# Half of the rope's squares go behind the block sums, and a table says how many rope slices follow each sum

## What is computed

```
h = _rmsnorm(x, norm_gain[l])
proj = h @ w_in[l]
q_a, k_a, v_a, g_a, q_b, k_b, v_b, g_b = jnp.split(proj, split_at, axis=-1)
q_a = _rmsnorm(q_a.reshape(b, s, A_HEADS, HEAD_DIM), q_norm_a[l])
k_a = _rmsnorm(k_a.reshape(b, s, A_KV_HEADS, HEAD_DIM), k_norm_a[l])
q_a = q_a * cos + _rotate_half_axial(q_a) * sin
k_a = k_a * cos + _rotate_half_axial(k_a) * sin
...
o_a = _gqa_blocked(q_a, k_a, v_a) * jax.nn.silu(g_a)
```

## Time and profile before

| what | value |
|---|---|
| three timed runs | 1477.88, 1477.89, 1478.12 us; median 1477.89 |
| the profiled execution's own time | 1478.08 us |
| span of its profile | 1476.3 us (1.78 us of the time lie around it) |
| PE busy | 1425.7 us, 97% of the span |
| DVE busy | 902.3 us, 61% |
| ACT busy | 631.1 us, 43% |
| POOL busy | 485.4 us, 33% |

### The profile page before, as it was taken

The page is one execution under the profiler, slowest core; times in us unless marked ns, Lnnn a source line. Parts: engine busy times, 40 slices in busy tenths (PEclk is TensorE's granted clock), DMA queues, the critical chain, the costliest instruction groups (busy, mean ns, idle before and its releaser), DMA issues.

```text
span 1476.3 us, 30658 instructions
## 1 busy us (share of the span) xinstructions
PE 1425.7 (97%) x12538; PEld 1257.1 (85%) x12538; DVE 902.3 (61%) x1535; ACT 631.1 (43%) x1251; POOL 485.4 (33%) x554
## 2 busy tenths in 40 slices
PE   7998989989999999999999999999998998999998
PEld 7998988867788788888899999888897887888887
DVE  6899971349999888745520633452424776888431
ACT  5422321137777677633432122332335554777210
POOL 0176641310000277622202212221205884434420
PEclk9999999999999999999999999999999999999999
DMA  6303346000000033256325245433121121222342
GB/s 234 115 15 94 101 152 123 29 1 1 1 1 1 28 116 95 81 178 180 85 44 59 54 91 94 53 64 50 30 69 41 31 90 43 66 81 63 101 134 80
DMA packets 89937, 109.50 MB, mean 74 GB/s; under 512 B 25215, under 2 KB 71967, under 8 KB 89800
## 3 DMA queue, kind: packets, MB, share of 16 engines
q1 hardware_dynamic: 89800, 107.55, 27.8%
HBM read 82.30 MB, written 25.22 MB: 73 GB/s over the span
## 4 chain that ended last, share of the span: by engine, by line
PE 58%; DVE 4%; ACT 1%; issue 1%; POOL 0%; DVEq 0%; ACTq 0%
PE ps L393 23%; PE ps L1812 12%; PE ps L3317 2%; PE ps L1620 2%; PE ps L1604 2%; PE ps L3303 2%; PE ps L3292 1%; PE ps L2693 1%; PE ps L2636 1%; PE ps L2651 1%; PE ps L1597 1%; PE ps L1598 1%; PE ps L1599 1%; PE ps L3280 1%; PE ps L3293 1%
## 5 line engine op out<-in xcount | busy, mean ns | idle before, releaser
L359 POOL TENSOR_TENSOR p_w_lo<-p_w_raw,p_w_hi 128x2048 fp32r<-128x2048 f32 (+1 forms) x21 | 103.5, 4927 | 394.0 <-ACT p_w_hi L332 394.0
L393 PE MATMUL ps<-p_w_hi,w_out_hi 128*128 128x256 f32 (+1 forms) x640 | 180.9, 283 | 0.1
L393 PE MATMUL ps<-p_w_lo,w_out_hi 128*128 128x256 f32 (+1 forms) x640 | 180.4, 282 | 0.0
L393 PE MATMUL ps<-p_w_hi,w_out_lo 128*128 128x256 f32 (+1 forms) x640 | 180.4, 282 | 0.0
L393 PEld LDWEIGHTS ps<-p_w_hi,w_out_hi 128*128 128x128 f32 x640 | 121.0, 189 | 0.9 <-issue 0.6
L393 PEld LDWEIGHTS ps<-p_w_hi,w_out_lo 128*128 128x128 f32 x640 | 121.1, 189 | 0.0
L393 PEld LDWEIGHTS ps<-p_w_lo,w_out_hi 128*128 128x128 f32 x640 | 120.4, 188 | 0.0
L332 ACT CAST p_w_hi<-p_w_raw 128x2048 fp32r<-128x2048 f32 (+1 forms) x22 | 42.0, 1909 | 124.1 <-DMA p_w_raw<-w_in 93.1
L1325 DVE TENSOR_TENSOR a_pt_lo<-ps,a_pt_hi 128x512 fp32r<-128x512 f32 x128 | 82.2, 683 | 15.3 <-ACT a_pt_hi L1376 15.3
L1376 ACT CAST a_pt_hi<-ps 128x512 fp32r<-128x512 f32 x128 | 68.9, 590 | 45.8 <-PE ps L1266 45.8
L1368 ACT ACTIVATE tok<-ps,a_stat 128x1024 f32<-128x1024 f32 x64 | 72.5, 1132 | 22.7 <-DVE a_stat L1320 22.7
(11 more groups left out here) (348 smaller groups left out, 4282.1 us busy)
## 6 DMA issues: line engine op xcount, KB each, us to landing
p_w_raw<-w_in SPq DMA_DIRECT2D x20, 1024.0 KB, 9.0
kbT<-x SPq DMA_DIRECT2D x8, 512.0 KB, 6.9
p_w_raw<-w_in SPq DMA_DIRECT2D x8, 512.0 KB, 4.3
b_w_raw<-w_out SPq DMA_DIRECT2D x8, 512.0 KB, 3.6
qT<-s_gate SPq DMA_DIRECT2D x8, 512.0 KB, 6.9
qT<-x SPq DMA_DIRECT2D x8, 512.0 KB, 3.5
s_x<-qT SPq DMA_DIRECT2D x8, 512.0 KB, 2.8
c_table<-s_line SPq DMA_DIRECT2D x8, 512.0 KB, 3.9
```

The lines of the kernel that those rows point to most:

```text
L359: ops.tensor_tensor(self.w_lo[:, b, :, 0:w], self.raw[:, :, 0:w], self.w_hi[:, b, :, 0:w].bitcast(F32), ALU.subtract).then_inc(self.w_lo_r ...
L393: last = self.nc.tensor.matmul(out, lhs, rhs, start=(kt == 0 and i == 0), stop=(kt == KT - 1 and i == 2))
```

## The change

The squares of tiles 0 to 3 and `place_second_sum` stay where they are. The squares of tiles 4 to 7 (with the scale behind the last) become a generator, `square`, chained ahead of `rope`, and the sums no longer wait for them. How many slices follow sum n is in a table: row 0 for group 0, row 1 for groups 1 and 2.

```
         pr.first_vector(dve, sv.first_sum)
         sv.prepare_vector(dve)
-        for t in range(NT):
-            if t == NT // 2:
-                sv.place_second_sum(dve, pr.chunk_end(STD - 1))
...
-        turning = rope(dve, step)
-        for _ in sv.evacuate(dve):
-            for _ in range(2):
-                next(turning, None)
-        for _ in turning:
+        squares = square(dve, step)
+        for t in range(NT // 2):
+            next(squares)
+        sv.place_second_sum(dve, pr.chunk_end(STD - 1))
+        work = one_after_other(squares, rope(dve, step))
+        for n, _ in enumerate(sv.evacuate(dve)):
+            for _ in range(SLICES[min(n // 10, 1)][n % 10]):
+                next(work, None)
+        for _ in work:
             pass
...
+    SLICES = ((1, 1, 0, 2, 0, 0, 1, 1, 1, 2), (2, 1, 0, 2, 1, 2, 2, 2, 2, 2))
+
+    def one_after_other(*works):
+        for work in works:
+            yield from work
+
+    def square(dve, step):
+        for t in range(NT):
+            dve.wait_ge(pr.emptied["act"], 2 * NT + t + 1)
+            x = qkv[:, t, 0:NH * HD]
+            step(nc.vector.tensor_tensor(tmp[:, :], x, x, ALU.mult))
+            step(nc.vector.tensor_reduce(stat[:, 0, t * NH:(t + 1) * NH],
+                                         tmp[:, :].rearrange("p (h d) -> p h d", d=HD), AX.X, ALU.add))
+            if t == NT - 1:
+                nc.vector.tensor_scalar(stat[:, 0, :], stat[:, 0, :], 1.0 / HD, EPS, ALU.mult, ALU.add).then_inc(var_ready, 1)
+            yield
```

## The result

The change makes the kernel faster by 0.73%: 1467.24 us (1466.04 to 1468.55, four runs) against 1477.97 us for the kernel before in the same session (1477.88 to 1478.12, four runs), a ratio of 0.9927 with a 95% interval of 0.991 to 0.9945. The profiled execution took 1467.59 us, its span 1465.8. The forecast was 1465.8 us, with a range of 1464.5 to 1470.5.

A forecast was written before the change was run, and what follows sets the result against it. PE, busy 97% of the span, was taken as the bound, with stalls waiting for DVE's L813. From 1478.08 us, 13.05 for both stalls came off and 0.8 for thin places was added: 1465.8 us, range 1464.5 to 1470.5.

The forecast's parts named there:

- The two stalls: PE's waits for L813 at product 4 of groups 0 and 2: both go, 13.05 us with their slow matmuls.
- The start of group 0: Ahead of product 4 of group 0: first L813 at about 106, wanted at 112.9, so the first stall goes.
- the margin of 0.9 us: Group 1's weights: second `low` ends at 135.0, PE wants it at 135.9; nothing charged, 2 us at most.
- Groups 1 and 2: Group 1's L813 at 149 to 153 and last L826 at 173 to 183; no stall there, second stall goes.
- its limit of 182.4: Latest start of group 1's last L826 that has STD's weights ready when PE wants them at 210.4.
- the part on the rest: After group 2: rope and L420 evictions hidden; second q_b chunk's L359 1.0 us ahead of PE, 1 us at most.
- all four thin places: Group 1's weights, its L813, STD's weights, second q_b chunk: each could lose up to 2 us; 0.8 charged in all.
- the likeliest case: Both stalls go and at most 2 us are lost: 1464.8 to 1467.3 us, chance 62%.
- Rival 1: A new stall of 1.5 to 5 us at L813 of group 1 or 2, or STD: 1467.5 to 1472, 23%.
- Rival 2: The stall at L813 of group 2 stays, DVE as far behind as before: 1470.6 plus up to 3, chance 6%.
- Rival 3: Little or no effect, squares still standing ahead of the first L813: 1475 to 1481 us, chance 4%.
- rival 4: DVE's backlog at group 1's last L826 delays STD's weights, making the kernel slower: 1481 to 1485 us, chance 3%.

The follow-up runs named there:

- experiment 5: The changed kernel itself run again, unedited, on a second chip: 1467.42 us, ratio 0.9927 to the kernel before.
- experiment 3: Changed kernel with the table undone: squares moved, but two slices behind every sum, as before; 1473.4 us, ratio 0.9975.
- 9: Changed kernel with three more slices ahead of the first L813 of group 1, taken from behind it; 1468.76 us, ratio 0.9934.
- 4: Changed kernel with all eight squares back ahead of the sums, only the slice table kept; 1473.81 us, ratio 0.9974.
- experiment 10: Changed kernel with group 2's two slices behind n = 26 split, one behind n = 25, one behind n = 27; 1464.39 us, ratio 0.9909.
- 1: Changed kernel with the two slices ahead of group 2's second L822 moved behind it; 1464.48 us, ratio 0.9912.
- 2: Changed kernel with the second q_b chunk's weight load issued ahead of the table loads on SP; 1464.7 us, ratio 0.9913.
- 6: Changed kernel with group 2's two slices behind its second L822 and the second q_b chunk's load ahead of the table loads; 1464.26 us, ratio 0.9905.
- 7: Changed kernel with four slices behind n = 26 and none behind n = 27, so four precede group 2's second L822; 1471.01 us, ratio 0.995.

## Why the prediction was right, and what it missed

**The two stalls.** Right, in mechanism and size: 13.05 us forecast, 13.31 measured. The forecast said that the changed profile would show no wait for L813 above 0.5 us; it shows none at all. It also said that there would be no window of half clock between 90 and 260, and that sign failed: the eight matmuls from 234.46 ran slow, with 0.79 granted over 232 to 240. STD's first matmul came at 209.79 (210 to 212 forecast), but the end did not move by as much: 13.7 us earlier at STD, 10.5 at the end.

**The start of group 0.** Right in kind. The DVE rows there:

```profile
98.75 0.69 DVE L806 TENSOR_TENSOR tok<-tok,ps 128x512 f32<-128x512 f32 x1 [0.81 <-ACT tok L777]
99.36 1.78 DVE L1111 TENSOR_TENSOR rope_tmp<-tok 128x640 f32<-128x640 f32 x1
...
104.96 0.69 DVE L813 TENSOR_TENSOR f_v<-tok,ps 128x512 f32<-128x512 f32 x1
106.94 0.69 DVE L813 TENSOR_TENSOR f_v<-tok,ps 128x512 f32<-128x512 f32 x1 [1.29 <-PE ps L766]
```

The first L813 came at 104.96 (106.1 forecast), the second at 106.94 and waiting for PE. The timelines of ACT and POOL, with the root, the fourth emptying of X and group 1's weights:

```profile
114.66 0.27 ACT L1039 ACTIVATE rope_stat<-rope_stat 128x80 f32<-128x80 f32 x1 [6.61 <-DVE rope_stat L1115]
118.47 0.38 ACT L786 ACTIVATE p_spill<-ps 128x256 f32<-128x256 f32 x1 [1.30 <-DMA s_gate<-p_spill]
...
127.25 2.98 POOL L627 TENSOR_TENSOR p_w_lo<-p_w_raw,p_w_hi 128x1024 fp32r<-128x1024 f32 x1
```

The root was at 114.66 ("near 115"). The second `low` ended at 130.2 where 135.0 was the worst and 132 to 135 the working value, so the margin of 0.9 us was 5.2 in fact (wanted at 89.60 + 8 x 5.72 = 135.4). The forecast's reason, that the wait for the store would take up a part of the delay, holds: ACT's fourth emptying of X started at 118.47 after 1.30 us where it had waited 4.27, so of the root's 4.3 us only 0.6 were left. Whether the store shared the DMAs with two weight loads, as the forecast had it, no run tests.

**Groups 1 and 2.** The pair of L813 of group 1 started at 148.65 (149 to 153 forecast), wanted from 152.5. The last L826 of group 1 started at 179.97. That is inside the stated 173 to 183 but past the 173 to 177 of the working, and 2.4 us ahead of its limit of 182.4. DVE's first and last sum of group 1:

```profile
139.37 0.69 DVE L806 TENSOR_TENSOR tok<-tok,ps 128x512 f32<-128x512 f32 x1
...
179.97 0.68 DVE L826 TENSOR_TENSOR tok<-tok,ps 128x512 f32<-128x512 f32 x1
```

Both times hold two misses that cancel, and that is luck. ACT's copy started at 138.58, earlier than the forecast's 141 to 145, and the slices were dearer than its 1.9 us. The three ahead of L813 took 8.1 us where 5.7 were charged. From L806 to L826 were 40.6 us where 32.0 were forecast; 3.5 of them DVE waited for PE, which leaves (40.6 - 3.5 - 5.4)/14 = 2.3 us a slice. From a copy at 141 to 145 the same way would have ended some 2.4 to 6.4 us later, about at the limit of 182.4 or past it, unless those 3.5 us of waiting had taken up a part. STD's weights were there at 201.58 + 4.60 = 206.2, 3.6 us early. The two L813 of group 2 came at 185.67 and 187.08, wanted from 192.6. There the forecast's sum has a slip: it names five slices and adds four. With five it is 11.3 us from L826, and the late end of 183 would have missed its 193.2 by 1. In the run POOL was idle from 179.30 to 185.17, so no slice was held up, and the whole way took 5.7 us.

**The term that was mis-sized** is the last of the part on the rest: "That L359 itself ends 1.0 us ahead of PE's job at 245.78 and hangs on SP's queue behind table loads that move with PE; I charge nothing, 1 us at most." The place was named and the slack was right (0.97). But what the loads move with is the `c12` store, and so DVE's L822, with PE only as long as no slice holds L822. The forecast looked at L806, L813 and L826 and never at L822, which in the trace of before waited 2.19 us for PE and so looked safe. Behind it the new table still has two slices between the two L822, where the rope of before had been used up after n = 24, and POOL's 4.6 us L359 falls just there. The part of the sum for all four thin places was 0.8 us; this one alone cost 3.9 in the profiled execution and 2.6 in another (experiment 5). From the profiled time of before, the sum with what was measured is 1478.08 - 13.31 - 0.38 + 3.88 - 0.7 = 1467.6, where 1467.59 was measured: 3.1 too little was charged, and 1.3 of it came back by more won (0.3), an earlier start (0.4) and the 0.7 elsewhere, none of which the forecast had a reason for. The median of 1467.24 lies just inside the likeliest case, 1464.8 to 1467.3, although that case's condition, at most 2 us lost, did not hold. That is luck.

**The rivals.** Rival 1 (a smaller new stall, "1467.5 to 1472") describes the size of the stall that came but not the place: it named L813 and STD. Experiments 3 and 9 show that its mechanism is real and near. Rival 2 (the second stall stays) is excluded: no wait. Rival 3 (little effect) and rival 4 (slower) did not come; experiments 3 and 4 show that it takes both halves to come near the whole gain.

**The shared port.** The Trainium skill (SBUF — State Buffer, "Who interferes with whom") says that a DVE instruction with two SBUF inputs and a POOL instruction that reads SBUF exclude each other for a whole instruction. The trace agrees: 4.63 us against 0.69 for one L1152, behind and ahead of POOL's L359 (changed kernel and experiment 10), while the sums that read PSUM kept 0.67 to 0.69 us throughout. The forecast's rival 1 and its late end priced what waits in group 1 with POOL's 2.4 us; at the place that mattered POOL's instruction is 4.6 us long.

## What to carry to other kernels

When work is spread behind signals, list every signal that something waits for, also those that had slack: the one that was lost here fed a store, and the store stood ahead of a weight load in an in-order DMA queue, some 27 us ahead of the matmul that in the end stood still. Price a filler by the longest instruction on the other engine that can catch it, not by its mean. And once two stalls are gone, compare each later hand-over's lead (here L822 to STD) with the kernel before: the idle time followed from it to 0.12 us.

## What the runs showed of the hardware that was not expected

**The clock after an idle time is not the same in two executions of one kernel.** The two profiles of the changed kernel have the same idle time at the same place (2.37 and 2.32 us). In the first, the granted clock was 0.79 over 232 to 240 us and 8 matmuls ran at the 1.2 GHz level, 1.5 us lost. In the second (experiment 5) the window over the same stretch has 1.00:

```profile
232.00:240.00 8.00, 5.84 (x26) 4.62 (x26) 0.69 (x1) 0.35 (x1) 3.31 (x3) 1.00 0.42 131
```

Over the profiles: after 5.31, 4.02 and 4.26 us of idle the lower level followed (22, 18 and 11 matmuls, 2.15, 1.57 and 2.2 us), and so it did after the stalls ahead of product 4 in experiments 3 (4.7 us) and 4 (3.45 us). After 2.24 to 2.41 us, at the second q_b chunk, it followed twice of four times; after 1.49 us there (experiment 3) it did not. So a stall of this size costs 1.1 times its own length or 1.6 to 1.8 times that; the forecast had used 1.4. The spread of the timed runs does not show this. The changed kernel's runs spread over 2.5 us where those of before, in the same session, spread over 0.24, but in the later sessions the kernel before spread over 1.6 to 3.0 us, and the versions without this idle time (1, 2, 6 and 10) over 1.1 to 3.2.

**The chain from L822 to the `low` of the next chunk is long and stiff.** From L822's start to the end of L359 were 26.8 us in the kernel before and in the changed one, 26.7 in experiments 3, 5, 7 and 9, 26.8 in 4 and 27.3 in 1 and 10, though most of it is DMA beside other traffic. In SP's queue of the changed kernel the table loads and `c21` stores hold the head for 4.75 and 6.94 us ahead of the weight load.
